# A one-core transformer step in fp32 on Trainium2: shorter routing, unread products, reordered waits, first weights in halves

## The chip, the cores and the metric

One core of a Trainium2 chip runs the whole program in one launch. The metric is device time in microseconds: the median of the runs, each from the first to the last instruction of the kernel.

## What is computed

The input is 256 tokens of width 1024 and a context of 256 tokens. The first block is an adaptively modulated layer with a gated delta net and a Fourier mixer, then a gated convolutional feed-forward. The second block has two layers: a short-convolution mixer or a linear recurrence, each followed by a mixture of 32 experts (two of one group of eight for each token) and a gate on an embedding. Cut to what matters for the change:

```python
mod_l = (silu_c @ w_ada[i] + b_ada[i])[:, None, :]
...
hl = modulate(rmsnorm(xl, g_pre_mix[i]), sh1l, sc1l)
hc = modulate(rmsnorm(xc, g_pre_mix[i]), sh1c, sc1c)
ul, zl, ql, kl, vl, bl, gl = mixer_inputs(hl, w_in[i], w_qkv_conv[i], a_log[i], dt_bias[i])
...
yl = mixer_out(ul, ol, zl, w_fourier[i], g_gdn[i], w_out[i])
xl = xl + gt1l * rmsnorm(yl, g_post_mix[i])
...
hl = modulate(rmsnorm(xl, g_pre_ffn[i]), sh2l, sc2l)
xl = xl + gt2l * rmsnorm(conv_ffn(hl, w_up[i], w_dwc[i], w_down[i], True), g_post_ffn[i])
...
pg = jax.nn.softmax((xf @ w_rg).astype(jnp.float32) + b_rg.astype(jnp.float32), axis=-1)
pg_top, g_top = lax.top_k(pg, 1)
le = ((xf @ w_re).astype(jnp.float32) + b_re.astype(jnp.float32)).reshape(n, N_GROUPS, EXPERTS_PER_GROUP)
le_sel = jnp.take_along_axis(le, g_top[:, :, None], axis=1)[:, 0]
...
hb = jax.nn.silu(xb @ w_gate[e]) * (xb @ w_up[e])
return hb @ w_down[e]
```

## The kernel before, in words

**Engines and semaphores.** Each engine has one hand-written instruction stream; semaphores join them. Activations lie transposed, as eight tiles (`k` = 0 to 7) of 128 channels by 256 tokens (512 with the context).

**Dense products.** A dense weight arrives by DMA in 2 MB chunks of 128x4096 (`w_in.0` is the first chunk of the mixer's input projection). ScalarE writes a rounded high part of each half chunk into ring slot 4 or 5 (L1403), and VectorE (L1980, `weights_low`) or GpSimd (L1865) then writes the remainder over the chunk; a table `by_dve` says which. The input is split in the same way: ScalarE writes the high part, VectorE the remainder (L1964, L1970, L2070). TensorE makes three products per `k` (`split_product`, L622): high by high, high by low, low by high. `projection` begins with `first_uses`, which takes `k` in the outer loop, so that each `k` needs only one new input tile; `together` says for how many of its two outputs both column tiles are made in that loop. The remaining outputs go through `dense_split`.

**The start.** TensorE computes the modulation (`ada_step`, L720 and L615), then the first uses of `w_in.0`, each `k` opened by three small rate products (L744, `ab_product`) for beta and decay. VectorE's order there is: scaled inputs of `k` 0 and 1 (L2075), the remainder of `w_in.0`'s first half, the low inputs of `k` 0 (L2070), and so on.

**The solve.** VectorE inverts a triangular matrix by a loop over columns and slips the modulation columns of later parts (`ada_columns`, L2201) in between; TensorE's `ada_step` products wait for these.

**Norms.** A residual is added tile by tile (L2005, L2008), ScalarE squares it (L1391), TensorE sums the squares over channels with a matrix of ones (L694), ScalarE makes the root (L1383, L1384), and VectorE and ScalarE make scaled, shifted, split inputs (L1993, L1426, L1412, L1964). The up-projection (`w_up`, 11 chunks) follows; its outputs go through a 3x3 convolution on VectorE. The down-projection has four pairs of output tiles, each tile of 22 steps of `k` (`n_k` = FT); `down_half` tells that the first tile's chunk is free.

**Experts.** In each of the two expert layers, 96 chunks of 2 MB (`q` = 0 to 95: per quad of four experts, four gates, four ups, four downs) run through ten places, in order, on one DMA queue issued by SyncE. `EXPERT_RINGS` says which place is which buffer; one place is made of two halves (`xnT` and `ple_w`), and its half in `ple_w` can be loaded only after the embedding products (`ple_mm`, L1054) have read it. Chunk `q` waits until chunk `q`-10 has been used (`consumed_by`). The first ten chunks are loaded while the mixer still runs. Routing lies between the mixer and the first gate product: logits (L1037), group and expert choice on VectorE (L2374 to L2412), ranks by products with a triangle of ones (L1083 to L1087), one-hot masks (L2429), and the gather of tokens by products (L1098). L1185 are the gate and up products, L1205 and L1262 products of the down-projections.

## Time and profile before

| | us |
|---|---|
| median of 3 runs (range) | 1683.92 (1681.86 to 1685.35) |
| the profiled execution | 1682.87 |
| its span in the trace | 1680.9 |
| TensorE busy | 1360.4 (81%) |
| VectorE busy | 593.0 (35%) |
| ScalarE busy | 433.9 (26%) |
| GpSimd busy | 219.8 (13%) |

The page says that the main DMA queue moved 525.22 MB and that the chain that ended last consists of TensorE for 53% and of DMA for 38%. Busy shares are means over stages with different limits. Idle time in brackets is time in which that engine had nothing to run, with what ended it.

### The profile page before, as it was taken

The numbers are of one execution on the slowest core, as the hardware profiler recorded it, in microseconds if no ns is written. First come the engines' busy times: TensorE is split into PE (matmuls) and PEld (weight loads), VectorE is DVE, ScalarE is ACT, GpSimd is POOL, SyncE is SP. The second block draws the span as 40 slices with busy tenths as digits, with TensorE's granted clock in tenths as the row PEclk, the third lists the DMA queues.
The fourth block names the chain that finished last, engine by engine and source line by source line (L and its number), as shares of the span: only waits on it lengthen the run. The fifth ranks groups of instructions, "written<-read, shape, count | busy, mean of one in ns | idle before, by whom it ended". The sixth has DMA issues, their size and how long they took to land.

```text
span 1680.9 us, 21875 instructions
## 1 busy us (share of the span) xinstructions
PE 1360.4 (81%) x9530; PEld 896.4 (53%) x9530; DVE 593.0 (35%) x1145; ACT 433.9 (26%) x655; POOL 219.8 (13%) x119
## 2 busy tenths in 40 slices
PE   5999998999999996776667567999966767666778
PEld 2797697999989961221222122998622212221226
DVE  2576723899437720110110011677201001101106
ACT  3445334544444320000000001665200000000005
POOL 0307322487430000000000000000000000000000
...
GB/s 402 127 59 164 202 113 201 115 187 154 157 216 151 373 316 428 427 428 426 427 428 425 429 425 412 232 163 362 273 427 427 427 426 428 426 427 427 427 410 99
DMA packets 51905, 528.40 MB, mean 314 GB/s; under 512 B 4704, under 2 KB 4832, under 8 KB 20064
## 3 DMA queue, kind: packets, MB, share of 16 engines
q1 hardware_dynamic: 51232, 525.22, 76.5%
...
HBM read 525.91 MB, written 1.05 MB: 313 GB/s over the span
## 4 chain that ended last, share of the span: by engine, by line
PE 53%; DMA 38%; DVE 4%; ACT 2%; SPq 2%; issue 1%; POOL 0%; DVEq 0%; ACTq 0%; POOLq 0%
PE bank L622 25%; DMA ring<-in_w_up 9%; PE bank L1185 9%; DMA ring<-in_w_gate 7%; DMA ring<-in_w_down 5%; DMA work<-in_w_down 5%; DMA work<-in_w_gate 5%; PE bank L1205 4%; DMA work<-in_w_up 4%; PE bank L1262 3%; PE bank L1330 2%; DMA ring<-in_dense 2%; PE bank L615 1%; PE bank L694 1%; SPq L524 1%; PE bank L1054 1%
## 5 line engine op out<-in xcount | busy, mean ns | idle before, releaser
L1185 PE MATMUL bank<-ring,work 128*32 128x512 f32 x1216 | 272.6, 737 | 142.3 <-DMA ring<-in_w_up 76.7
L622 PE MATMUL bank<-work_rounded,ring_rounded 128*128 128x256 f32 (+1 forms) x2032 | 317.8, 291 | 6.4 <-DVE xn_rounded L1970 3.5
L622 PEld LDWEIGHTS bank<-work_rounded,ring_rounded 128*128 128x128 f32 x2032 | 277.4, 189 | 15.9 <-issue 5.8
L622 PE MATMUL bank<-xn_rounded,ring_rounded 128*128 128x256 f32 (+1 forms) x1472 | 255.0, 291 | 3.4 <-DVE xn_rounded L1964 3.4
L1185 PEld LDWEIGHTS bank<-ring,work 128*32 128x32 f32 x1216 | 58.5, 131 | 322.2 <-issue 118.9
L622 PEld LDWEIGHTS bank<-xn_rounded,ring_rounded 128*128 128x128 f32 x1472 | 209.0, 194 | 7.7 <-issue 4.5
L2501 DVE TENSOR_TENSOR work<-work,bank 128x512 f32<-128x512 f32 x16 | 11.0, 689 | 569.8 <-PE bank L1185 569.8
L1865 POOL TENSOR_TENSOR ring_rounded<-ring,ring_rounded 128x2048 fp32r<-128x2048 f32 (+1 forms) x37 | 159.5, 4330 | 205.7 <-ACT ring_rounded L1403 205.7
L1185 PE MATMUL bank<-work 128*32 128x512 f32 x496 | 142.9, 688 | 32.7 <-DMA work<-in_w_gate 17.4
L1932 POOL TENSOR_TENSOR work<-work_rounded,work 128x128 f32<-128x128 f32 x32 | 12.1, 401 | 1071.5 <-PE bank L1237 738.6
L1403 ACT ACTIVATE ring_rounded<-ring 128x2048 fp32r<-128x2048 f32 (+1 forms) x78 | 136.5, 1796 | 51.5 <-PE bank L622 27.4
L1185 PE MATMUL bank<-spare,work 128*32 128x512 f32 x224 | 120.2, 738 | 22.3 <-DMA spare<-in_w_gate 14.6
L1205 PE MATMUL bank<-ring,work 128*32 128x512 f32 x576 | 100.6, 638 | 20.5 <-DMA ring<-in_w_down 20.5
L1980 DVE TENSOR_TENSOR ring_rounded<-ring,ring_rounded 128x2048 fp32r<-128x2048 f32 (+1 forms) x41 | 88.7, 2190 | 49.3 <-ACT ring_rounded L1403 49.1
L1185 PE MATMUL bank<-xn,work 128*32 128x512 f32 x112 | 73.4, 840 | 29.3 <-DMA work<-in_w_gate 20.0
L1725 ACT ACTIVATE work<-bank 128x512 f32<-128x512 f32 x16 | 9.6, 597 | 294.1 <-PE bank L1185 294.1
L1730 ACT ACTIVATE work<-bank 128x512 f32<-128x512 f32 x14 | 8.4, 600 | 293.5 <-PE bank L1098 293.5
L1205 PE MATMUL bank<-work 128*32 128x512 f32 x304 | 74.6, 649 | 11.5 <-DMA work<-in_w_down 11.5
L1185 PEld LDWEIGHTS bank<-work 128*32 128x32 f32 x496 | 32.5, 124 | 91.6 <-issue 44.0
L2511 DVE SCALAR_TENSOR_TENSOR xn_rounded<-bank,work,work_rounded 128x512 fp32r<-128x512 f32 x32 | 24.0, 751 | 160.0 <-ACT work_rounded L1738 160.0
L2293 DVE SCALAR_TENSOR_TENSOR work<-bank,params,work 128x189 f32<-128x189 f32 (+2 forms) x176 | 76.0, 432 | 6.2
L1098 PEld LDWEIGHTS bank<-work_rounded,work 128*128 128x128 f32 x512 | 58.5, 192 | 11.8 <-issue 11.7
...
## 6 DMA issues: line engine op xcount, KB each, us to landing
...
```

The costliest lines, as they stand in the source:

```text
L524: sp.dma_start(expert_columns(q, CHUNK // 4 * e, CHUNK // 4).rearrange("p (j n) -> p j n", j=2), columns[e])\
L622: last = mm(out, rv(high_store[r][:, at:at + P]), rv(x[part][k]), start=opens and k == 0 and j == 0, stop=closes and k == n_k - 1 and j == 2)
L1098: last = mm(out, xtok[:, u, k], rv(oneh[:, u].rearrange("p x s -> p (x s)")).bitcast(F32), start=u == 0, stop=u == NH - 1)
L1185: ins = mm(out[slots(y), :], xg[:, k, slots(y)], expert_columns(w, at, 512), start=k == 0, stop=k == KT - 1)
L1205: ins = mm(bank[6 + half][slots(y), :], hidT[:, j, slots(y)], expert_columns(w, at, 512), start=j == 0, stop=j == 3)
L1262: last = mm(bank[(use + b) % BANKS][:, SEQ * i:SEQ * i + SEQ], w[:, at:at + P], x[:, k], start=k == i == 0, stop=k == KT - 1 and i == 1)
L1330: last = mm(bank[(USE["out_b"] + b) % BANKS][:, SEQ * i:SEQ * i + SEQ], w[:, at:at + P], rr[0][:, k], start=k == i == 0, stop=k == KT - 1 ...
L1403: signal(act.activation(rv(high_store[HIGH_SLOT[n]][:, a:b]), w[:, a:b], ACT.Copy), "w_high")
L1865: pool.tensor_tensor(rv(w), w, rv(high_store[HIGH_SLOT[n]][:, a:b]), ALU.subtract).then_inc(S["w_low"], 1)
L1980: v.tensor_tensor(rv(w), w, rv(high_store[HIGH_SLOT[n]][:, a:b]), ALU.subtract).then_inc(S["w_low_dve"], 1)
L2293: ins = v.scalar_tensor_tensor(dst, x[:, r0 + dy:r1 + dy, c0 + dx:c1 + dx], par("w_dwc", 9 * f + 3 * (dy + 1) + dx + 1, 1), dst, ALU.mult, ...
L2511: ins = v.scalar_tensor_tensor(rv(y_low[half]), bank[6 + half][:].rearrange("p (k t) -> p k t", k=2), slot_w, rv(y_high[half]).rearrange(" ...
```

## The change

1. `w_in.0` is loaded as two DMAs of one half each (`half_full` tells the first); the remainder of its second half is made by GpSimd.
2. The rate weights' high and low parts lie side by side, so each `k` has two products of 32 rows; a product with a constant `fold` adds the two halves of the rows and transposes them.
3. `idle_products(n)`: TensorE makes n products of constants whose result nobody reads: 6 ahead of the first uses, 4 and 2 around the sums of squares ahead of the up-projection, 3 ahead of the short-convolution mixer (15 in all).
4. The mixer's output projection has `together=2`.
5. In the first pair of the down-projection, steps 0 to 19 of both tiles come before steps 20 and 21 of both.
6. In the norm ahead of the up-projection, ScalarE writes only the high part (with the shift in its bias), and VectorE makes the low part in one instruction.
7. Modulation columns move to earlier places around the solve.
8. Routing: the tokens are the stationary operand, so the logits come out with tokens in rows; the copy, the transposes and several VectorE steps go. The rank products are signalled after three of five, the weights come after the first one-hot masks, and only two of the eight column tiles of the embedding products stay ahead of the first gate; the other six follow the first quad's ups.
9. Place 5 is now ring 5 and place 9 the two halves; the second half of `q` = 9 waits for the embedding products in the loop, ahead of `q` = 14. A few small waits and signals follow from this.

```diff
-EXPERT_RINGS = (0, 1, None, None, None, None, 2, 4, 3, 5)
+EXPERT_RINGS = (0, 1, None, None, None, 5, 2, 4, 3, None)
...
-    halved = tuple(first[f"ple{layer}"] for layer in range(2))
-    whole = (*halved, first["w_in_b"])
+    halved = (first["w_in"], *(first[f"ple{layer}"] for layer in range(2)))
+    whole = (*halved[1:], first["w_in_b"])
...
-        ("w_in", (0, 3, 4)), ("w_out", (1,)), ("w_up", (1,)), ("w_in_a", range(1, 6)), ("w_out_a", range(2)), ("ple0", (1,)),
+        ("w_in", (3, 4)), ("w_out", (1,)), ("w_up", (1,)), ("w_in_a", range(1, 6)), ("w_out_a", range(2)), ("ple0", (1,)),
...
-    by_dve += [(first["w_down"] + c, 0) for c in range(2, 8)] + [(first["w_in_a"], 0)]
+    by_dve += [(first["w_in"], 0)] + [(first["w_down"] + c, 0) for c in range(2, 8)] + [(first["w_in_a"], 0)]
...
             sp.wait_ge(S["tok_mm"], 4 * (layer + 1))
-            expert(5, 0)
-            sp.wait_ge(S["ple_mm"], 4 * (layer + 1))
-            expert(5, 1)
+            expert(9, 0)
...
+                if q == EXPERT_SLOTS + TOGETHER:
+                    sp.wait_ge(S["ple_mm"], EMBEDS * (layer + 1))
+                    expert(9, 1)
...
+            both = ready is not None and n_k == FT
+            parts = (range(n_k - 2), range(n_k - 2, n_k)) if both else (range(n_k),)
+            for part in parts:
+                for i, (chunk, tile) in enumerate(tiles):
+                    for k in part:
...
+        def idle_products(count):
+
+            for _ in range(count):
+                mm(bank[6][:], ones, consts[:, 0:4 * P], start=True, stop=True)
+
...
+        idle_products(6)
...
-            for j, (w, x) in enumerate(((0, 0), (0, 1), (1, 0))):
-                last = mm(bank[7][0:16, :], rv(w_ab[w][:, k]), rv(both[x][k]), start=k == 0 and j == 0,
-                          stop=k == KT - 1 and j == 2)
+            for x in range(2):
+                last = mm(bank[7][0:32, :], rv(w_abs[:, k].rearrange("p s c -> p (s c)")), rv(both[x][k]), start=k == 0 and x == 0,
+                          stop=k == KT - 1 and x == 1)
...
         sum_squares(late)
+        idle_products(4)
         ready = norm_input()
+        idle_products(2)
         projection("up", "w_up", FT, xparts, ready, together=1)
...
-                last = mm(bank[7][0:36, 0:SEQ], w_r[:, layer, k], xs[k], start=k == 0, stop=k == KT - 1)
+                for u in range(NH):
+                    last = mm(bank[6][:, LOGITS * u:LOGITS * u + LOGITS], xs[k][:, P * u:P * u + P], w_r[:, layer, k],
+                              start=k == u == 0, stop=k == KT - 1 and u == 1)
...
+                    signal(v.scalar_tensor_tensor(rv(xnT[:, k - 2]), xnT[:, k - 2], mod[:, 24 + k - 2, 0:1], rv(rounded[:, k - 2]),
+                                                  ALU.add, ALU.subtract), "xn_ready")
...
-            if k == 4:
-                weights_low(FIRST["w_in"], (1,))
...
-        for m in range(1, 5):
-            ada_columns(2, m)
+        for m in range(2, 5):
+            columns_added(2, m)
```

**What moves on VectorE and GpSimd at the start.** The names: `ring0` is `w_in.0`, whose high parts lie in `ring4`; `xn` and `hT` with `gains` are the scaled inputs, `xn_rounded<-xn,mod,work_rounded` the low inputs of a `k` (two instructions for each `k`). VectorE before:

```order
L1980 TENSOR_TENSOR ring0_rounded_49<-ring0,ring4_rounded_53 128x2048 [waits w_high]
L2070 SCALAR_TENSOR_TENSOR xn_rounded_55<-xn,mod,work_rounded_57 128x256 [waits x_high]
L2070 SCALAR_TENSOR_TENSOR xn_rounded_55<-xn,mod,work_rounded_57 128x256
L2075 SCALAR_TENSOR_TENSOR xn<-work,gains,bank5 128x256
L2075 SCALAR_TENSOR_TENSOR xn<-hT,gains,bank5 128x256
L2070 SCALAR_TENSOR_TENSOR xn_rounded_55<-xn,mod,work_rounded_57 128x256 [waits x_high]
L2070 SCALAR_TENSOR_TENSOR xn_rounded_55<-xn,mod,work_rounded_57 128x256
L2075 SCALAR_TENSOR_TENSOR xn<-work,gains,bank5 128x256
L2075 SCALAR_TENSOR_TENSOR xn<-hT,gains,bank5 128x256
L1980 TENSOR_TENSOR ring0_rounded_49<-ring0,ring4_rounded_53 128x2048 [waits w_high]
L2070 SCALAR_TENSOR_TENSOR xn_rounded_55<-xn,mod,work_rounded_57 128x256 [waits x_high]
```

VectorE now:

```order
L1995 TENSOR_TENSOR ring0_rounded_49<-ring0,ring4_rounded_53 128x2048 [waits w_high]
L2088 SCALAR_TENSOR_TENSOR xn_rounded_55<-xn,mod,work_rounded_57 128x256 [waits x_high]
L2088 SCALAR_TENSOR_TENSOR xn_rounded_55<-xn,mod,work_rounded_57 128x256
L2093 SCALAR_TENSOR_TENSOR xn<-work,gains,bank5 128x256
L2093 SCALAR_TENSOR_TENSOR xn<-hT,gains,bank5 128x256
L2088 SCALAR_TENSOR_TENSOR xn_rounded_55<-xn,mod,work_rounded_57 128x256 [waits x_high]
L2088 SCALAR_TENSOR_TENSOR xn_rounded_55<-xn,mod,work_rounded_57 128x256
L2093 SCALAR_TENSOR_TENSOR xn<-work,gains,bank5 128x256
L2093 SCALAR_TENSOR_TENSOR xn<-hT,gains,bank5 128x256
L2088 SCALAR_TENSOR_TENSOR xn_rounded_55<-xn,mod,work_rounded_57 128x256 [waits x_high]
```

The second remainder has left VectorE's queue, where it stood behind the low inputs of `k` 1 and 2. GpSimd's queue at its start, now:

```order
L1867 MEMSET work 128x256
L1879 ISA
L1879 TENSOR_TENSOR ring0_rounded_49<-ring0,ring4_rounded_53 128x2048 [waits w_high]
L1879 TENSOR_TENSOR ring1_rounded_50<-ring1,ring5_rounded_54 128x2048 [waits w_high] x2
L1879 TENSOR_TENSOR ring2_rounded_51<-ring2,ring4_rounded_53 128x2048 [waits w_high] x2
```

It stands there first, ahead of the four remainders of the next two chunks, which were first before.

**What moves on TensorE around the norm ahead of the up-projection.** `bank4<-xn,consts` are the sums of squares, `xn_rounded_55,ring5_rounded_54` the first products of the up-projection. Before:

```order
L694 MATMUL bank4<-xn,consts 128x256
L694 MATMUL bank4<-xn,consts 128x256 [waits sq_ready]
L694 MATMUL bank4<-xn,consts 128x256
L694 MATMUL bank4<-xn,consts 128x256 [waits sq_ready]
L694 MATMUL bank4<-xn,consts 128x256
L694 MATMUL bank4<-xn,consts 128x256 [waits sq_ready]
L694 MATMUL bank4<-xn,consts 128x256
L694 MATMUL bank4<-xn,consts 128x256 [waits sq_ready]
L694 MATMUL bank4<-xn,consts 128x256
L622 MATMUL bank2<-xn_rounded_55,ring5_rounded_54 128x256 [waits xn_ready,w_low,dense_free3,dense_free2]
```

Now:

```order
L718 MATMUL bank6<-consts 128x512 x4
L708 MATMUL bank4<-xn,consts 128x256 [waits sq_ready]
L708 MATMUL bank4<-xn,consts 128x256
L708 MATMUL bank4<-xn,consts 128x256 [waits sq_ready]
L708 MATMUL bank4<-xn,consts 128x256
L708 MATMUL bank4<-xn,consts 128x256 [waits sq_ready]
L708 MATMUL bank4<-xn,consts 128x256
L708 MATMUL bank4<-xn,consts 128x256 [waits sq_ready]
L708 MATMUL bank4<-xn,consts 128x256
L718 MATMUL bank6<-consts 128x512 x2
L632 MATMUL bank2<-xn_rounded_55,ring5_rounded_54 128x256 [waits xn_ready,w_low,dense_free3,dense_free2]
L632 MATMUL bank2<-xn_rounded_55,ring5_rounded_54 128x256
```

The two rows `bank6<-consts`, of four and of two products, are new; the others keep their order.

**What moves on TensorE in the routing of the first expert layer.** `bank5<-work,consts 128x32` are ranks, `work_rounded_57,work 128x128` the gather, `work 128x256` the embedding products, `ring0,work` the first gate. Before:

```order
L1054 MATMUL bank7<-work 128x256 x4
L1083 MATMUL bank5<-work,consts 128x32 [waits mask_ready]
L1084 MATMUL bank5<-work,consts 128x32
L1085 MATMUL bank5<-work,consts 128x32
L1086 MATMUL bank5<-work,consts 128x32
L1087 MATMUL bank5<-work,consts 128x32
L1054 MATMUL bank0<-work 128x256 [waits tok_sb]
L1054 MATMUL bank0<-work 128x256 x3
L1098 MATMUL bank2<-work_rounded_57,work 128x128 [waits onehot,tok_sb]
L1098 MATMUL bank2<-work_rounded_57,work 128x128 x7
L1098 MATMUL bank3<-work_rounded_57,work 128x128 x8
L1054 MATMUL bank6<-work 128x256 x4
```

Now:

```order
L1078 MATMUL bank4<-work 128x256 [waits ple_w_load,mask_load]
L1078 MATMUL bank4<-work 128x256
L1100 MATMUL bank5<-work,consts 128x32 [waits mask_ready]
L1101 MATMUL bank5<-work,consts 128x32
L1102 MATMUL bank5<-work,consts 128x32
L1103 MATMUL bank7<-work,consts 128x32
L1104 MATMUL bank7<-work,consts 128x32
L1113 MATMUL bank2<-work_rounded_57,work 128x128 [waits onehot,tok_sb]
L1113 MATMUL bank2<-work_rounded_57,work 128x128 x7
L1113 MATMUL bank3<-work_rounded_57,work 128x128 x8
L1078 MATMUL bank6<-work 128x256 x2
```

Ahead of the first of these rows before stands another pair of embedding tiles (`bank4`, four instructions). Of the four pairs that stood ahead of the first gate, two single tiles are left there (two instructions each); the other six follow the first quad's ups.

## Rows read from the trace of the kernel before

**Rows 1.** The page: gigabytes per second in 40 slices of the span.

```profile
GB/s 402 127 59 164 202 113 201 115 187 154 157 216 151 373 316 428 427 428 426 427 428 425 429 425 412 232 163 362 273 427 427 427 426 428 426 427 427 427 410 99
```

**Rows 2.** The chain that ended last, the first products: start, length, work.

```profile
24.40 12.37 DMA ring<-in_dense
...
45.89 0.69 PE bank L744 x3
46.58 1.39 PE bank L622 x6
```

**Rows 3.** Timeline of the start: start, length, engine, line, tiles, [idle before <- releaser].

```profile
36.80 1.91 ACT L1403 ACTIVATE ring_rounded<-ring 128x2048 fp32r<-128x2048 f32 x1 [12.99 <-DMA ring<-in_dense]
...
38.74 2.29 DVE L1980 TENSOR_TENSOR ring_rounded<-ring,ring_rounded 128x2048 fp32r<-128x2048 f32 x1 [2.02 <-ACT ring_rounded L1403]
40.21 1.90 ACT L1403 ACTIVATE ring_rounded<-ring 128x2048 fp32r<-128x2048 f32 x1
40.95 0.88 DVE L2070 SCALAR_TENSOR_TENSOR xn_rounded<-xn,mod,work_rounded 128x256 fp32r<-128x256 f32 x2
...
41.97 0.58 PE L744 MATMUL bank<-work_rounded 128*16 128x512 f32 x1 [7.52 <-DVE xn_rounded L2070]
```

**Rows 4.** Windows: busy (x instructions) by engine, granted clock, DMA share, GB/s.

```profile
18.00:21.00 3.00, 3.00 (x7) 1.18 (x7) 0.00 (x0) 0.00 (x0) 0.00 (x0) 1.00 1.01 431
297.00:300.00 3.00, 3.00 (x16) 3.00 (x15) 2.33 (x7) 2.69 (x9) 0.00 (x0) 0.50 0.00 0
```

**Rows 5.** Timeline behind the triangular solve, TensorE.

```profile
194.82 2.02 PE L615 MATMUL bank<-consts,work 128*128 128x128 f32 x16 [1.79 <-DVE mod L2201]
```

**Rows 6.** Timeline ahead of the second half of the mixer's output projection.

```profile
246.30 4.54 POOL L1865 TENSOR_TENSOR ring_rounded<-ring,ring_rounded 128x2048 fp32r<-128x2048 f32 x1
...
249.06 3.06 DVE L1964 TENSOR_TENSOR work_rounded<-work,work_rounded 128x256 fp32r<-128x256 f32 x4 [4.28 <-ACT work_rounded L1412]
...
258.64 3.55 PE L622 MATMUL bank<-work_rounded,ring_rounded 128*128 128x256 f32 x28 [1.45 <-DVE work_rounded L1964]
```

**Rows 7.** Timeline around the norm ahead of the up-projection.

```profile
285.74 6.51 PE L694 MATMUL bank<-xn,consts 128*128 128x256 f32 x16 [3.57 <-ACT xn L1391]
...
289.03 0.63 ACT L1391 ACTIVATE xn<-hT 128x512 f32<-128x512 f32 x1 [0.43 <-DVE hT L2008]
...
295.61 9.61 PE L622 MATMUL bank<-xn_rounded,ring_rounded 128*128 128x256 f32 x56 [3.36 <-DVE xn_rounded L1964]
```

**Rows 8.** The chain through the up-projection.

```profile
295.61 129.91 PE bank L622 x1056
```

**Rows 9.** Timeline at the start of the down-projection.

```profile
434.01 11.19 PE L622 MATMUL bank<-work_rounded,ring_rounded 128*128 128x256 f32 x92 [1.47 <-DVE work_rounded L1964]
...
435.10 2.66 ACT L1403 ACTIVATE ring_rounded<-ring 128x1408 fp32r<-128x1408 f32 x2 [2.40 <-PE bank L622]
```

**Rows 10.** Windows at the short-convolution mixer's first projection, columns as in rows 4.

```profile
493.00:496.00 3.00, 0.19 (x1) 0.00 (x0) 1.89 (x6) 1.32 (x3) 0.00 (x0) 1.00 0.72 306
496.00:499.00 3.00, 2.30 (x11) 2.33 (x12) 3.00 (x10) 2.22 (x5) 0.00 (x0) 0.54 0.74 311
```

**Rows 11.** Timeline of the first expert layer's routing and first experts.

```profile
602.49 3.62 PE L1054 MATMUL bank<-work 128*128 128x256 f32 x16
...
605.38 0.23 DVE L2412 TENSOR_TENSOR work<-work 128x64 f32<-128x64 f32 x1
...
608.78 3.73 PE L1098 MATMUL bank<-work_rounded,work 128*128 128x128 f32 x32
...
614.18 3.64 PE L1185 MATMUL bank<-ring,work 128*32 128x512 f32 x32
614.28 0.38 SPq L533 DMA_DIRECT2D work<-in_w_up  x1
...
616.16 2.06 SPq L536 DMA_DIRECT2D ring<-in_w_down  x2
```

**Rows 12.** The same place in the second expert layer.

```profile
1206.44 3.64 PE L1185 MATMUL bank<-ring,work 128*32 128x512 f32 x32
```

240 lines of the change are left out of this document (116 added, 124 removed).

## Prediction

> **What bounds the kernel now.** I read first how many bytes move when [rows 1]. In slices 16 to 24 and 30 to 38 the DMA queue moves 427 GB/s: these are the two expert layers, and there the kernel ends as early as its stream of 2 MB chunks does, 4.92 us for each. Elsewhere the chain that ended last is TensorE's work with a few waits in it. So two kinds of edit can gain: one that shortens a wait of TensorE outside the expert layers, and one that makes the expert stream start earlier. A us saved in TensorE's work inside the stream is worth nothing. Then I read the chain and the timeline at each place that the change touches: at the start, the wait for `w_in.0` [rows 2, 3]; behind the solve [rows 5]; in the output projection [rows 6]; around the norm and the up-projection [rows 7, 8]; at the down-projection [rows 9]; at the next mixer [rows 10]; and in the routing [rows 11, 12]. A saving ahead of an expert layer passes through it whole, since the stream goes on when places come free.
>
> **The start.** Before, `w_in.0` lands at 36.77 [rows 2]; ScalarE's high part starts at 36.80, VectorE's remainder at 38.74, the low inputs at 40.95, TensorE at 41.97 after 7.52 us idle [rows 3]. The DMA engines are full there (431 GB/s [rows 4]), so a half of 1 MB takes 2.43 us and the first half lands at 34.35. ScalarE: 1.91 to 36.25. VectorE's scaled inputs are done by then (its order starts the remainder behind four of them), remainder 36.75 to 39.05, low inputs 0.88 to 39.95: TensorE starts at 40.0, 2.0 earlier. The six unread products fill 34.45 to 39.6: seven records of such a product fit in 3.00 us [rows 4], two records each, so 0.86 each, 5.2 in all. They cost nothing as long as the input is not earlier than 39.6.
>
> Now the second half. ScalarE starts its high part 3.41 after the first (36.80 to 40.21 [rows 3]), so at 37.8, to 39.7. GpSimd then makes its remainder, 4.54 us by [rows 6], from 39.9 to about 44.4. What is beside it: VectorE's low inputs of `k` = 1, due at 40.7, which read two operands from SBUF. In [rows 6] four such instructions begin at 249.06 and take 3.06 us, and GpSimd's remainder ends at 250.84: 1.78 us of them are the wait for GpSimd, the four themselves 1.28, 0.32 each. So I let the low inputs of `k` = 1 wait until 44.4 and end at 45.25, and TensorE starts `k` = 1 at 45.3, after 3.4 us idle. The other steps: a `k` takes 2.08 now, 0.69 for three rate products and 1.39 for six others [rows 2]; with two rate products 1.85. End of the first uses: 45.3 + 7 x 1.85 = 58.25, against 41.97 + 3.92 + 7 x 2.08 = 60.45 (the first `k` takes 3.92 at the low clock, 41.97 to 45.89). Gain 2.2; if the idle time brings the clock down again, one `k` costs 1.84 more and 0.36 is left. Idle stretches of about that length do bring it down elsewhere: the 3.36 us ahead of 295.61 are followed by a granted clock of 0.50 (1.2 GHz) [rows 4, 7]. I take **0.4**, near that end. Without the wait for GpSimd TensorE never stops: 40.0 + 8 x 1.85 = 54.8, gain 5.65. Bounds 0 and 5.65.
>
> The Trainium skill has a rule that speaks against this edit ("SBUF — State Buffer", section "Who interferes with whom"): a VectorE instruction with two SBUF inputs and a GpSimd instruction that reads SBUF exclude each other, and the later one is blocked for the whole of the earlier one. The trace agrees [rows 6]. By that rule the start gains 0.4 to 2.2; with two engines that don't disturb each other it would be 5.65, and the whole sum 18.8.
>
> **Behind the solve.** TensorE's 1.79 us ahead of 194.82 are a wait for the modulation columns L2201, which stand on VectorE behind the two large transposes [rows 5]. Now they are made inside the column loop, before them; the loop gets one in and gives one up. TensorE goes straight on: **1.8**. If the solve's own results are late next, less; bounds 1.2 and 1.8.
>
> **Output projection.** The 1.45 us ahead of 258.64 wait for the fifth `cat` tile [rows 6]. `together=2` puts 24 products more ahead of that wait, at 129.91 / 1056 = 0.123 us each [rows 8] 2.9 us of work that was to do anyway: **1.45**. Bounds 1.0 and 1.45.
>
> **Norm and up-projection.** Three terms. (a) The sums of squares take 6.51 us for eight products (16 records) behind 3.57 us idle, at the low clock [rows 7]. With four unread products (3.4 us) inside those 3.57 the clock stays high; then the end is set by the last squares, 289.03 + 0.63 = 289.66, plus the last four records, 0.24 each: 290.6 instead of 285.74 + 6.51 = 292.25. Gain 1.65. (b) The chain from the root to the first low input loses one ScalarE pass and a handover. A pass over 512 columns takes 0.63 [rows 7]; for 256 and the handover together I estimate 0.65. (c) 56 products take 9.61 us from 295.61; at 0.12 each (129.91 less these 2.9 us, over 1056) it would be 6.75. VectorE's low inputs come every 0.9 us at most (two instructions a `k`, 0.44 each by the pair of 0.88 in [rows 3]) against 1.08 us of TensorE's nine products per `k`, so TensorE keeps its pace. Gain 2.8 if two unread products (1.7 of the 2.7 us gap that is left) keep the clock up. Together **5.1**; bounds 2.3 (a and b alone, or c alone) and 5.3.
>
> **Down-projection.** The 1.47 us ahead of 434.01 [rows 9] are now filled by the second tile's steps, but the first tile ends later: before at 434.01 + 6 x 0.12 = 434.7; now at 432.54 + 60 x 0.12 + 0.7 = 440.45. Behind it waits ScalarE's high part of the third chunk (435.10, waiting for TensorE; 1.33 each), then VectorE's remainder of 1408 columns (2.29 x 1408 / 2048 = 1.6 by [rows 3]), then the second pair. 440.8 + 1.33 + 1.6 = 443.8. Before, the second pair starts at 434.01 + 72 x 0.12 = 442.6. So the wait comes back larger: **-1.2**. Bounds -3 (the clock drops in the 2.6 us gap) and +1.4.
>
> **Next mixer.** From 496.7, 11 products take 2.30 us at a mean clock of 0.54 [rows 10], and the idle time before is over 3 us; at 0.12 they take 1.3, and some more follow at the low clock: **1.3** if the three unread products (2.6 us) hold it. Bounds 0 and 1.5.
>
> **Routing, twice.** The first gate product starts at 614.18 [rows 11]. Ahead of the mask (605.38) go the logits' copy, two transposes and some seven VectorE instructions of its size (0.23): seven of 0.2 and some 0.7 for copy, transposes and handovers put the mask at about 603.4. Three rank products, ranks and one-hot masks take 1.9 (608.78 less 605.6, less the 1.3 for which the gather stood behind embedding products): gather from 605.3, 3.73 long, then one tile of embedding products (3.62 for four tiles, 0.9): gates at 610.0, 4.2 earlier. But what counts is the stream. Before, SyncE issues the second half of its split chunk at 614.28 and `q` = 10 at 616.16, behind it; 614.31 + 2.46 = 616.77 is when the stream proper can start. Now `q` = 10 goes 1.98 us behind the first gate, at 612.0, with nothing ahead; the half chunk comes later, inside the stream: 612.0 + 2.46 = 614.4. Gain 2.35, not 4.2. The second layer has the same pattern, gates at 1206.44 [rows 12]: **4.7** together. Its condition: all chunks from 14 on queue behind SyncE's wait for the embedding products. These end at 610.0 + 13.8 (four times 3.45 [rows 11]) + 5.3 = 629.1; chunks 10 to 13 keep the queue busy until 612.0 + 4 x 4.92 = 631.7. 2.6 us to spare. Bounds per layer 0 and 4.2.
>
> **Nothing for the rest.** The wider parameters (some 45 KB) are 0.1 us; the transposes by `fold` replace four others; the moved split in the up stage has TensorE-bound work over it.
>
> **Sum.** 0.4 + 1.8 + 1.45 + 5.1 - 1.2 + 1.3 + 4.7 = 13.55 us. The terms are from an execution of 1682.87 us (span 1680.9), which is 1.05 below the median of the runs, 1683.92. In that frame: 1670.4.
>
> **Rivals.** A: the low inputs don't wait for GpSimd at the start. For it: later low inputs in the trace are often made without harm, and the wait needs the overlap at just this place. Against: [rows 6]. 5.25 more (5.65 for 0.4): **1665.1**, chance 0.15. B: the unread products don't hold the clock (too few for the gaps that are left). Then (c) 2.8 and the next mixer's 1.3 are lost and the down-projection's gap costs 1 more: 8.45 gained, **1675.5**, chance 0.2. For it: the clock is still 0.5 from 297 to 300, well after TensorE has resumed. The Trainium skill ("TensorE: Matmul & The Clock Gate", Part 1, "What's actually happening") says that the lower clock is the default and that activity of the array releases it; unread products should then do as well as others, which no row here shows. C: the mask is earlier by less, or the embeddings end some 2 us late, and the stream starts as before: 4.7 lost, **1675.1**, chance 0.06. D, the slower side: SyncE's wait ahead of `q` = 14. If ScalarE frees the banks of the six late tiles only behind the first quad's hidden products, the queue runs dry in both layers. Each us beyond the 2.6 to spare costs one per layer; the change is slower by over 0.2% (3.4 us, about what a measurement of this kernel can tell from none) from 11 us late on. At 12 us late: 13.55 - 2 x 9.4 = 5.3 slower, **1689.2**, chance 0.03. For it only that the wait is new; against, that ScalarE has 0.60 us copies there and little else. E: the terms eat each other up and less than 3.4 us is left: 0.03. The forecast keeps 0.53.
>
> **Range.** The forecast's own is 1667 to 1674. With A and B in it: 1662.5 to 1677.5 holds some 8 in 10. Faster 0.93, within 0.2% 0.04, slower 0.03.
>
> **What would show it.** At the start: GpSimd's remainder beside low inputs that take some 4 us, TensorE idle over 3 us behind the first `k`, first uses ending at 58 to 60. L2201's wait and the 1.45 us gone. The granted clock near 1 from 290 to 300 in the norm. A wait of some 2.6 us ahead of the second pair of the down-projection. First gate some 4 us nearer to the last logits, `q` = 10 right behind, no gap in the queue at `q` = 14. I am wrong most likely at the start (A), at the clock, or where a wait that I took for hidden comes out.

## The result and the profile after

| | before | after |
|---|---|---|
| median (range), us | 1683.92 (1681.86 to 1685.35) | 1674.47 (1673.04 to 1677.23) |
| the profiled execution, us | 1682.87 | 1675.44 |
| its span, us | 1680.9 | 1673.3 |

The ratio of the medians is 0.9947, with a 95% interval of 0.9933 to 0.996: 9.45 us faster, where 13.55 was forecast. The profiled execution of before was 1.05 below its median, that of after is 0.97 above, so the two traces show only 7.6 us. Page of after (busy time of the engines, granted clock in tenths, GB/s in 40 slices):

```profile
PE 1377.9 (82%) x9584; PEld 914.9 (55%) x9584; DVE 592.4 (35%) x1130; ACT 432.0 (26%) x647; POOL 225.4 (13%) x120
...
PEclk9999889999999997887887788999988878878889
...
GB/s 402 131 55 161 211 106 210 151 166 140 166 209 152 376 327 427 426 429 428 428 427 429 427 426 413 237 160 361 284 428 428 428 428 427 428 427 426 428 412 109
```

The expert stream is as full as in [rows 1]; it begins earlier. I laid the starts of the same TensorE instruction in the two traces beside each other; "lead" is how much earlier it starts now, "own part" how much of that arose since the row above.

| place (time in after) | lead, us | its own part | forecast |
|---|---|---|---|
| end of the first uses (59.65) | 0.85 | 0.85 | 0.4 |
| modulation products behind the large transposes (191.94) | 2.88 | +2.0 | +1.8 |
| output projection (252.3) | 0.03 | -2.85 | 0 |
| sums of squares end (280.87) | 1.31 | +1.3 | +1.45 |
| up-projection, two `k` on (295.4) | 5.5 | +4.2 | +5.1 |
| down-projection, third pair (458) | 2.8 | -2.7 | -1.2 |
| next mixer, first products (494.40, then 496) | 2.3, then 3.3 | -0.5, +1.0 | 0, +1.3 |
| first routing, gather (604.64) | 4.1 | +1.36, and -0.5 ahead of it | +2.35 |
| second routing, gather (1194.84) | 6.2 | +1.30, and +0.8 ahead of it | +2.35 |
| end (1673.3) | 7.6 | +1.4 | 0 |

The own part of a routing is what the stretch from the first one-column sum to the first gather product got shorter: 21.73 to 20.37 us, and 17.84 to 16.54.

Two rows need care. The 0.85 us of the start don't last: at 159.8 both traces stand level (159.79 before, 159.81 now). The 2.88 at 191.94 come from behind that place: a wait of 1.65 us for modulation columns at 168.39 is gone (lead 1.9), a wait for a DMA of 0.81 at 175.24 is new (lead 1.0), and the 1.79 of [rows 5] are gone. And a lead is the difference of two single executions, which differ by themselves. Seven traces of this study, that of after among them, share every instruction of the changed start: their eighth `k` (`k` = 7) begins anywhere from 56.00 to 59.03. The product in the row of 252.3 begins at 251.1 to 255.1 in the six of them that share the solve too, and at 251.1 to 253.1 in the four traces with the old start and solve. So ahead of that row the change gains nothing that these traces show.

**The start.** Timeline of after, columns as in [rows 3]:

```profile
34.46 5.32 PE L718 MATMUL bank<-consts 128*128 128x512 f32 x12
...
36.81 2.28 DVE L1995 TENSOR_TENSOR ring_rounded<-ring,ring_rounded 128x2048 fp32r<-128x2048 f32 x1
...
39.73 4.55 POOL L1879 TENSOR_TENSOR ring_rounded<-ring,ring_rounded 128x2048 fp32r<-128x2048 f32 x1 [38.68 <-ACT ring_rounded L1422]
...
40.03 0.39 PE L763 MATMUL bank<-work_rounded 128*32 128x512 f32 x1 [0.26 <-DVE xn_rounded L2088]
...
40.59 4.38 DVE L2088 SCALAR_TENSOR_TENSOR xn_rounded<-xn,mod,work_rounded 128x256 fp32r<-128x256 f32 x2
...
45.02 0.42 PE L763 MATMUL bank<-work_rounded 128*32 128x512 f32 x1 [3.00 <-DVE xn_rounded L2088]
```

The two low inputs of `k` = 1 take 4.38 us instead of 0.88 [rows 3]: they end 0.7 behind GpSimd's remainder. TensorE stands still for 3.00 us.

**The granted clock.** Windows of after, columns as in [rows 4]:

```profile
42.00:45.00 3.00, 0.03 (x1) 0.00 (x0) 3.00 (x3) 0.00 (x0) 2.29 (x1) 1.00 1.00 426
45.00:48.00 3.00, 2.98 (x8) 2.10 (x9) 3.00 (x8) 1.55 (x4) 0.00 (x0) 0.59 1.01 431
...
199.00:202.00 3.00, 2.57 (x73) 2.60 (x75) 0.54 (x1) 1.38 (x4) 2.88 (x5) 0.53 0.03 5
...
283.00:286.00 3.00, 2.54 (x9) 1.02 (x8) 3.00 (x9) 1.26 (x2) 0.00 (x0) 1.00 0.92 393
...
289.00:292.00 3.00, 2.25 (x7) 0.89 (x5) 1.55 (x4) 1.85 (x5) 0.00 (x0) 1.00 0.00 0
...
298.00:301.00 3.00, 3.00 (x28) 3.00 (x27) 2.96 (x2) 2.98 (x3) 0.00 (x0) 1.00 0.00 0
435.00:438.00 3.00, 0.55 (x5) 0.35 (x3) 1.63 (x1) 3.00 (x4) 0.34 (x1) 1.00 0.66 188
438.00:441.00 3.00, 2.88 (x13) 2.92 (x14) 1.15 (x1) 3.00 (x4) 3.00 (x1) 0.52 1.00 371
493.00:496.00 3.00, 2.06 (x15) 1.63 (x14) 3.00 (x10) 2.06 (x4) 0.00 (x0) 1.00 0.92 393
496.00:499.00 3.00, 3.00 (x27) 2.97 (x26) 3.00 (x9) 2.27 (x5) 0.00 (x0) 1.00 0.01 5
...
586.00:589.00 3.00, 3.00 (x26) 3.00 (x26) 0.00 (x0) 0.00 (x0) 0.00 (x0) 0.88 1.01 416
589.00:592.00 3.00, 3.00 (x17) 3.00 (x17) 0.00 (x0) 0.00 (x0) 0.00 (x0) 0.55 0.64 258
...
446.00:458.00 12.00, 12.00 (x102) 12.00 (x101) 1.62 (x1) 4.94 (x6) 3.40 (x1) 1.00 0.47 143
```

Three readings. Around the norm and in the next mixer the clock is now 1.00, where it was 0.50 and 0.54 [rows 4, 10]. Behind the two idle gaps (42 to 45, 435 to 438) it falls to 0.59 and 0.52, that is to 1.2 GHz for most of the window. The second fall is in all eight traces with that gap; the first is not in each: in experiments 4 and 9 the same idle time of 2.99 us stands at the same place, and the clock stays at 1.00, as the first line of the window rows of experiment 4 shows. And it falls in the routing (589 to 592) although TensorE is busy all the time. Before, the same window reads

```profile
589.00:592.00 3.00, 3.00 (x19) 2.01 (x18) 0.00 (x0) 0.00 (x0) 0.00 (x0) 1.00 1.03 423
```

**Norm and down-projection.** The chain of after that ended last:

```profile
292.40 127.68 PE bank L632 x1059
...
434.93 1.39 ACT ring_rounded L1422
...
436.34 1.64 DVE ring_rounded L1995
...
438.12 33.40 PE bank L632 x264
...
473.24 15.83 PE bank L632 x132
```

The up-projection starts 3.2 earlier (1.3 of that from the output projection) and takes 2.2 less than in [rows 8] (127.68 for three records more). Ahead of 438.12 stands the new wait of 2.57 us, exactly the two passes of which the prediction spoke.

**Solve and routing.** Timeline of after:

```profile
191.94 2.05 PE L625 MATMUL bank<-consts,work 128*128 128x128 f32 x16
...
192.69 1.28 ACT L1456 ACT_TABLE_LOAD   x1
...
194.88 3.93 PE L910 MATMUL bank<-ring,xn 32*32 32x32 f32 x128 [0.89 <-DVE ring L2236]
...
195.06 1.28 ACT L1456 ACT_TABLE_LOAD   x1
...
198.69 1.07 ACT L1586 ACTIVATE ring<-bank 32x512 f32<-32x512 f32 x2
...
199.43 0.23 PE L922 MATMUL bank<-ring 32*32 32x32 f32 x1 [0.62 <-ACT ring L1586]
...
585.98 1.96 PE L1060 MATMUL bank<-params,xn 128*128 128x40 f32 x16
...
604.64 3.81 PE L1113 MATMUL bank<-work_rounded,work 128*128 128x128 f32 x32 [0.57 <-DVE work_rounded L2428]
...
609.28 3.64 PE L1199 MATMUL bank<-ring,work 128*32 128x512 f32 x32
...
611.26 2.04 SPq L545 DMA_DIRECT2D ring<-in_w_down  x2
```

At 191.94 the wait of [rows 5] is gone. But the solve's own results are next: VectorE's second transpose (0.89 us), then ScalarE with two table loads of 1.28 us (0.62 us). The first gate is 4.90 earlier than in [rows 11], `q` = 10 too, 1.98 behind it as before.

### The profile page after: what moved, and what is told of

Its sections match the earlier page's. It is cut to its first block, busy times and chain, and to the rows that moved or that the text cites. A ratio compares the mean times of both kernels' runs of the same rounds, so it can differ in the third digit from the quotient of the medians.

```text
span 1673.3 us, 21964 instructions
## 1 busy us (share of the span) xinstructions
PE 1377.9 (82%) x9584; PEld 914.9 (55%) x9584; DVE 592.4 (35%) x1130; ACT 432.0 (26%) x647; POOL 225.4 (13%) x120
## 3 DMA queue, kind: packets, MB, share of 16 engines
q8 instruction: 78, 1.28, 0.3%
HBM read 525.95 MB, written 1.05 MB: 315 GB/s over the span
## 4 chain that ended last, share of the span: by engine, by line
PE 54%; DMA 38%; SPq 3%; ACT 2%; DVE 2%; issue 1%; POOL 0%; DVEq 0%; ACTq 0%; POOLq 0%
PE bank L632 26%; PE bank L1199 9%; DMA ring<-in_w_up 7%; DMA work<-in_w_gate 7%; DMA ring<-in_w_down 7%; DMA ring<-in_w_gate 5%; DMA work<-in_w_down 4%; DMA ring<-in_dense 4%; PE bank L1219 4%; DMA work<-in_w_up 4%; SPq L533 3%; PE bank L1281 3%; PE bank L625 2%; PE bank L1349 2%; PE bank L819 1%; PE bank L708 1%
## 5 line engine op out<-in xcount | busy, mean ns | idle before, releaser
L1199 PE MATMUL bank<-ring,work 128*32 128x512 f32 x1248 | 319.8, 727 | 134.0 <-DMA ring<-in_w_up 71.9
L632 PE MATMUL bank<-work_rounded,ring_rounded 128*128 128x256 f32 (+1 forms) x2032 | 322.1, 294 | 3.5 <-DVE ring_rounded L1995 2.6
L632 PEld LDWEIGHTS bank<-work_rounded,ring_rounded 128*128 128x128 f32 x2032 | 282.0, 193 | 12.4 <-issue 5.9
L1199 PEld LDWEIGHTS bank<-ring,work 128*32 128x32 f32 x1248 | 70.2, 130 | 306.0 <-issue 109.4
L1879 POOL TENSOR_TENSOR ring_rounded<-ring,ring_rounded 128x2048 fp32r<-128x2048 f32 (+1 forms) x38 | 165.2, 4364 | 196.5 <-ACT ring_rounded L1422 196.3
L1199 PE MATMUL bank<-work 128*32 128x512 f32 x480 | 153.9, 687 | 31.3 <-DMA work<-in_w_gate 15.7
L1219 PE MATMUL bank<-ring,work 128*32 128x512 f32 x576 | 127.8, 677 | 18.4 <-DMA ring<-in_w_down 18.4
L1199 PE MATMUL bank<-spare,work 128*32 128x512 f32 x224 | 115.5, 716 | 17.8 <-DMA spare<-in_w_gate 7.7
L1219 PE MATMUL bank<-work 128*32 128x512 f32 x304 | 88.8, 662 | 12.1 <-DMA work<-in_w_down 12.1
L1199 PE MATMUL bank<-xn,work 128*32 128x512 f32 x96 | 69.7, 884 | 25.7 <-DMA work<-in_w_up 14.2
L1199 PEld LDWEIGHTS bank<-work 128*32 128x32 f32 x480 | 37.3, 124 | 92.5 <-issue 46.2
L1752 ACT ACTIVATE work_rounded<-bank,work 128x512 fp32r<-128x512 f32 x32 | 22.0, 688 | 166.3 <-PE bank L1219 166.3
```

What stands on the lines that cost most here:

```text
L632: last = mm(out, rv(high_store[r][:, at:at + P]), rv(x[part][k]), start=opens and k == 0 and j == 0, stop=closes and k == n_k - 1 and j == 2)
L1199: ins = mm(out[slots(y), :], xg[:, k, slots(y)], expert_columns(w, at, 512), start=k == 0, stop=k == KT - 1)
L1219: ins = mm(bank[6 + half][slots(y), :], hidT[:, j, slots(y)], expert_columns(w, at, 512), start=j == 0, stop=j == 3)
L1879: pool.tensor_tensor(rv(w), w, rv(high_store[HIGH_SLOT[n]][:, a:b]), ALU.subtract).then_inc(S["w_low"], 1)
```

## The experiments

Each kernel was run beside the kernel before (whose median was 1682.9 to 1683.5), 4 to 12 executions each. The interval of a ratio is about 2 us to either side, and medians of two kernels within some 2 us aren't told apart, so for small edits I read the trace at the place too; a trace shows one execution.

**1. The two-tile order in the down-projection undone.**

```diff
-            both = ready is not None and n_k == FT
+            both = False
```

> Only the order of the first down-projection pair goes back to that of before. Theory 1 (the edit costs, since the first tile's chunk comes free later and the wait comes back as a larger one with a clock drop behind it): the 2.2 us or so of idle time ahead of the second pair go, 1.5 us come back ahead of steps 20 and 21, TensorE is 2 to 3 us earlier in the next mixer, and the whole is 2 to 3 us faster than the changed kernel, near 1672. Theory 2 (the loss there belongs to the earlier arrival of TensorE at that place, whatever the order): no difference beyond 1 us.

Measured: 1672.43, ratio 0.9941 (0.9928 to 0.9953): 2.0 below the changed kernel. Timeline, TensorE:

```profile
430.15 16.10 PE L632 MATMUL bank<-work_rounded,ring_rounded 128*128 128x256 f32 x132 [1.31 <-DVE work_rounded L1979]
```

The 1.31 us ahead of the last steps are back, no wait follows, and the clock doesn't fall. Counted from the first product of the up-projection, the next mixer starts 199.3 us on, against 202.0 in the changed kernel: this part of the change loses 2.7 us, where the forecast said 1.2. The median agrees (2.0), though by itself it wouldn't be clear of the noise.

**2. The second remainder of `w_in.0` back on VectorE.**

```diff
-        ("w_in", (3, 4)), ...
+        ("w_in", (0, 3, 4)), ...
+            if k == 4:
+                weights_low(FIRST["w_in"], (1,))
```

> w_in.0 is still loaded in halves, but the remainder of the second half is made by VectorE, at the place in its order where it stood before. Theory 1 (GpSimd's remainder blocks VectorE's low inputs for 4 us and brings TensorE's clock down): the low inputs of k = 1 take 0.9 us and not 4.4, TensorE goes on after its first k, and the first uses end at about 55.5, against 59.7 in the changed kernel. Theory 2 for what it is worth in the end: the 4 us pass through, near 1670.5; its rival: other waits ahead of the delta net take it up, as they took up 0.9 us in the changed kernel, and the whole is within 1.5 us of the changed kernel.

Measured: 1672.69, ratio 0.9945 (0.9932 to 0.9958), span 1670.8. Timeline:

```profile
40.90 0.87 DVE L2090 SCALAR_TENSOR_TENSOR xn_rounded<-xn,mod,work_rounded 128x256 fp32r<-128x256 f32 x2
...
42.19 0.39 PE L763 MATMUL bank<-work_rounded 128*32 128x512 f32 x1
```

The low inputs of `k` = 1 take 0.87 us again, TensorE doesn't wait (42.19 instead of 45.02), `k` = 7 starts 2.84 earlier, and in this trace 2.5 us of it reach the end. The 4.38 us are GpSimd's doing. What they cost in the end is less sure: `k` = 7 starts 1.2 to 4.2 earlier than in the seven traces named above, the row of 252.3 (249.99 here) 1.1 to 5.1 earlier than in the six, and the medians differ by 1.8.

**3. The fifteen unread products left out** (nobody reads them, so the output is the same).

```diff
-            for _ in range(count):
+            for _ in range(0):
```

> All 15 unread products are left out. Theory 1 (they hold the clock around the norm and ahead of the next mixer, and cost nothing): granted clock 0.5 again from some 3 us after the start of the gap ahead of the sums of squares, the up-projection's first 56 products 9.6 us again, 4 to 5.5 us slower than the changed kernel, near 1679.5. Theory 2 (the clock comes back by itself or they hide nothing): within 1 us of the changed kernel.

Measured: 1676.05, ratio 0.9963 (0.9951 to 0.9975): 1.6 above the changed kernel, far less than the 1679.5 of my theory. Windows:

```profile
45.00:48.00 3.00, 2.90 (x13) 2.16 (x14) 3.00 (x9) 1.47 (x4) 0.00 (x0) 1.00 1.02 437
...
283.00:286.00 3.00, 3.00 (x11) 2.44 (x10) 2.27 (x7) 1.67 (x3) 0.00 (x0) 0.65 0.14 60
...
292.00:295.00 3.00, 3.00 (x27) 3.00 (x27) 2.55 (x7) 2.44 (x4) 0.00 (x0) 1.00 0.00 0
493.00:496.00 3.00, 3.00 (x17) 3.00 (x16) 3.00 (x9) 1.78 (x4) 0.00 (x0) 0.55 0.12 44
```

Without them the clock is 0.65 under the sums of squares and 0.55 in the next mixer. The mixer pays for it: 91.4 us from its first product to the first one-column sum, against 89.9. The norm doesn't: from the row of 252.3 to the first product of the up-projection it is 40.18 us, against 40.08, since the last squares set the end of the sums. And the up-projection starts at full clock all the same. So in this trace the 2.8 us that the prediction gave to the clock in the up-projection need no unread product. With them the clock is 1.00 there in ten traces of ten; without them it is low in the three with the old norm (before, experiment 5 and `a2_before_fill`) and not here, so a single trace carries this reading. The start says nothing on them: `k` = 7 begins at 56.13 here, and at 56.00 in experiments 4 and 9, which have the unread products.

**4. One unread product of 512 columns between the sums and the router's products.**

```diff
+            idle_products(1, 7)
```

> One unread product of 512 columns stands between the one-column token sums and the router's 40-column products, at both places of both layers (four in all, 3.4 us of TensorE). Theory 1 (the stretches of one-column and 40-column products alone let the clock fall, which costs about 1.5 and 0.9 us in each layer): with them the granted clock stays near 1 from the first router products to the gather, and the time is 0 to 2 us better than the changed kernel in spite of the added work. Theory 2 (the clock falls for another reason): the clock falls as before and it is 2 to 3.4 us slower.

Measured: 1680.43, ratio 0.9987 (0.9975 to 0.9998), 6 us above the changed kernel. Windows:

```profile
45.00:48.00 3.00, 3.00 (x14) 2.22 (x15) 3.00 (x8) 1.59 (x4) 0.00 (x0) 1.00 1.02 437
...
589.00:592.00 3.00, 3.00 (x16) 3.00 (x16) 0.00 (x0) 0.00 (x0) 0.00 (x0) 0.50 0.19 78
```

The clock fell all the same and for longer (0.59, 0.50, 0.77 in the three windows from 586, 0.88, 0.55, 1.00 without). This remedy is refuted. It adds 3.4 us of TensorE work by its own count. The rest is the lower clock: in the second layer it stays at 0.50 from 1185 to 1200, and sums to gather take 23.18 us instead of 16.54. (The traced execution is 3.4 us above the median of its kernel.)

**5 to 7. Parts alone: only the routing on the kernel before; everything but the routing; only the norm's edits (unread products 4 and 2, high part only on ScalarE) on the kernel before.** The first takes over

```diff
-EXPERT_RINGS = (0, 1, None, None, None, None, 2, 4, 3, 5)
+EXPERT_RINGS = (0, 1, None, None, None, 5, 2, 4, 3, None)
...
+                for u in range(NH):
+                    last = mm(bank[6][:, LOGITS * u:LOGITS * u + LOGITS], xs[k][:, P * u:P * u + P], w_r[:, layer, k],
...
+                if q == EXPERT_SLOTS + TOGETHER:
+                    sp.wait_ge(S["ple_mm"], EMBEDS * (layer + 1))
```

> The kernel before with the routing part alone (items 8 and 9: logits, routing steps, embeddings, the swapped places). Theory 1 (each layer's stream starts 2.4 us earlier by the prediction's account, and some 3.2 by the changed kernel's trace, although the router's narrow products let the clock fall): 5 to 7 us faster than before. Theory 2 (the clock loss eats the routing gain and the time comes from elsewhere): within 2.5 us of before.

> The changed kernel without the routing part (all that stands ahead of the first expert layer's routing). Theory 1 (the parts add up; ahead of routing only some 3 us are left of the 8.85 forecast): 2 to 4 us faster than before. Theory 2 (the forecast's 8.85 us ahead of routing are there and the routing part is what falls short): 7 to 9 us faster than before.

> The kernel before with the edits around the norm ahead of the up-projection alone (four and two unread products, one ScalarE pass less). Theory 1 (the prediction's: sums 1.65, chain 0.65, clock 2.8): 4.5 to 5 us faster than before, granted clock near 1 from 285 to 303. Theory 2 (the clock there depends on where its falls and rises lie, and comes back without help in some executions, as it did in the kernel without unread products): 2 to 3 us faster.

Measured: only the routing 1676.80 (ratio 0.9961, 0.9948 to 0.9975); without the routing 1673.88 (0.9944, 0.993 to 0.9957); only the norm 1679.97 (0.9982, 0.9973 to 0.9991). The gains, about 6.5 and 9.5, add up to 16 where the whole has 9. In the trace the routing alone is worth 2.9 us (sums to gather 20.18 and 16.52 us against 21.73 and 17.84). The norm's edits bring the up-projection 3.24 us forward, then 5.46 behind its first products; 1.29 of both were there at the row of 252.3 already, so their own worth is 1.95, then 4.2, as in the whole. So the local terms do add up; something else sets the medians, and it is not in the list of the change.

**8. Where the `work` area lies.** The moving operands of the output and down-projections lie in one SBUF area, `work`, allocated behind the parameters. Wider parameters push it back, by 4 bytes a column: in the changed kernel by 88 columns. The distances between the starts of such products, at a granted clock of 1.00, go with the place, but not with it alone. The last column is the fourth pair of output tiles, which reads the same operand behind some products for the sums of squares:

| kernel | `work` further on than before, bytes | mean distance at 450 to 465, ns | products in 446 to 458 | mean distance in the fourth pair, ns |
|---|---|---|---|---|
| before | 0 | 118.7 | 104 | 117.3 |
| only the norm | 0 | 117.3 | 104 | 117.3 |
| `a2_before_fill` | 32 | 113.3 | 108 | 117.8 |
| without routing | 64 | 118.3 | 104 | 118.3 |
| only routing | 288 | 113.3 | 108 | 113.3 |
| changed kernel | 352 | 120.0 | 102 | 120.0 |
| `a1_shift192` | 544 | 113.3 | 109 | 113.3 |
| all remedies (experiment 11) | 544 | 113.3 | 109 | 113.3 |

In the experiments on the changed kernel that leave the place alone it is 120.0 again, in both columns. The up-projection reads `xn`, which is allocated ahead of the parameters, and has a median of 120.0 in every kernel. Two of the kernels in the table were made for this question; they change the place of `work` and of what is allocated behind it, and nothing that is computed: `a1_shift192` is the changed kernel with `gains` allocated ahead of `work` and eight unread constant columns (192 bytes), `a2_before_fill` the kernel before with the eight columns (32 bytes).

```diff
-    ("iota1", SLOTS), ("eps", 1),
+    ("iota1", SLOTS), ("eps", 1), ("fill", 8),
```

> The changed kernel with the large work area moved up by 192 bytes in SBUF (a small tile allocated ahead of it, and 8 unread columns of constants); not one instruction more or less. In the traces so far the dense products of 256 columns that read that area follow each other every 118.7 ns in the kernel before, every 120.0 in the changed kernel and its variants, and every 113.3 in the one with routing alone, where that area stands 288 bytes from its place before; here it stands at the same place modulo 256. Theory 1 (the place of the moving operand sets the pitch): 113.3 ns in the down-projection's steady part, 2 to 4 us faster than the changed kernel. Theory 2 (the instruction stream or the execution sets it): 120.0 ns, no difference beyond 1 us.

> The kernel before with 8 unread columns of constants more, which moves the work area by 32 bytes, to the same place modulo 256 as in the kernel with routing alone. Theory 1 (place sets the pitch): 113.3 ns in the down-projection, 2 to 4 us faster than before. Theory 2: 118.7 ns as before, no difference beyond 1 us.

Measured: a1 1672.15, ratio 0.9933 (0.992 to 0.9947), 2.3 below the changed kernel; a2 1680.94, ratio 0.9989 (0.998 to 0.9998), some 2 us below the kernel before. Both have a distance of 113.3 ns from 450 to 465. Window and chain of a2, then chain of a1:

```profile
446.00:458.00 12.00, 12.00 (x108) 12.00 (x108) 1.63 (x1) 5.01 (x6) 5.19 (x2) 1.00 0.49 151
...
472.30 15.55 PE bank L622 x132
```

```profile
438.91 31.49 PE bank L632 x264
...
472.13 14.98 PE bank L632 x132
```

The same 396 records take 46.47 us here and 49.23 in the changed kernel (33.40 and 15.83 above): 2.76 us with nothing changed but where buffers lie. a2 against the kernel before, which compute the same, shows it too in the first three pairs (108 products against 104; 38.37 us for 336 records against 40.14), but not in the fourth: 15.55 us for 132 records against 15.49, where `a1_shift192` and the routing alone take 14.98. And the kernel before has two distances, 118.7 and 117.3, with the operand at one place. So a move of the buffers changes the distance by up to 6.7 ns, and all seven traces at 352 bytes have 120.0 throughout; but within one execution a stretch can take another value than the one ahead of it, and what picks it isn't known.

**9. Router products between dense ones.**

```diff
-                dense_split(*tiles(b), x)
+                jobs = ahead() if ahead and b == uses - 1 else []
+                dense_split(*tiles(b), x, jobs=jobs)
...
+                        if jobs and k % 2 == 1 and not (i and k == n_k - 1):
+                            jobs.pop(0)()
```

> The changed kernel with its first layer's early token sums and router products put one by one between the dense products of the last output tile, and one group of token transposes between the late router products and the late token sums in both layers. No work is added. Theory 1 (rows of narrow products one after another let the clock fall): in the first layer the granted clock stays near 1 from 583 to 600 and TensorE is 1.5 to 2.5 us earlier at the first gate; 1.5 to 2.5 us faster than the changed kernel. Theory 2 (the narrow products lower the clock even when they are mixed with wide ones, or something else does): no gain, or less than 0.5 us.

Measured: 1675.09 (1673.35 to 1678.84), ratio 0.9959 (0.9946 to 0.9973). Windows:

```profile
589.00:592.00 3.00, 3.00 (x27) 3.00 (x27) 0.00 (x0) 0.00 (x0) 0.00 (x0) 1.00 0.67 272
```

The clock stays at 1.00 from 583 to 601, and sums to gather take 17.64 and 14.82 us, 2.7 and 1.7 less than in the changed kernel (in the second layer only the token products stand between the router's). That looks like theory 1, but it isn't shown. The clock falls later instead, to 0.58 from 604 to 607, in the gather itself:

```profile
602.92 5.44 PE L1118 MATMUL bank<-work_rounded,work 128*128 128x128 f32 x32 [0.57 <-DVE work_rounded L2433]
```

The gather takes 5.44 us instead of 3.81, and the first gate starts at 609.18, against 609.28 in the changed kernel. And the kernel of experiment 10, whose routing is that of the changed kernel, with 16 one-column and 16 40-column products in a row from 587.09 to 590.6, has the same shape without any product moved:

```profile
589.00:592.00 3.00, 3.00 (x28) 3.00 (x28) 0.00 (x0) 0.00 (x0) 0.00 (x0) 1.00 1.01 416
```

There sums to gather take 18.00 and 14.86 us, and its gather too takes 5.44. From the first sum to the first gate it is 23.90 and 19.46 us in experiment 9, 24.27 and 19.50 in experiment 10, 25.01 and 21.18 in the changed kernel. So how often the clock falls in a layer's routing, and where, differs between executions of the same instructions, and the mixed order isn't shown to be worth anything. The profiled span is 2.1 us shorter than that of the changed kernel, the median no shorter.

**10. The modulation columns back in their old places.**

```diff
-        columns_added(1, 1)
...
-            if j in (9, 14, 18):
-                columns_added(1, (9, 14, 18).index(j) + 2)
-            if j == 28:
-                columns_added(2, 1)
+            if j in (1, 9, 14, 18):
+                ada_columns(1, (1, 9, 14, 18).index(j) + 1)
```

> The changed kernel with the modulation columns at their old places around the solve (item 7 undone). Theory 1 (ScalarE's two table loads and its copies behind the modulation products set the end of the solve, so moving VectorE's columns gains nothing but an earlier fall of the clock in the 32x32 products): TensorE waits 1.8 us for the columns again, the first products that read the solved halves start within 0.3 us of where they do in the changed kernel, and the time is within 1 us of it. Theory 2 (the prediction's: the wait was worth 1.8 us): 1.5 to 2 us slower, near 1676.

Measured: 1675.45, ratio 0.9962 (0.9948 to 0.9975), 1.0 above the changed kernel, which the runs can't tell from it. Timeline, TensorE:

```profile
168.52 2.08 PE L625 MATMUL bank<-work 128*128 128x128 f32 x8 [2.54 <-DVE mod L2219]
...
202.05 0.18 PE L922 MATMUL bank<-ring 32*32 32x32 f32 x1 [1.06 <-ACT ring L1586]
```

I expected less than 0.3 us at the place and was wrong: the columns at their old places make TensorE wait at 168.52, and the products behind the solve start 2.62 later than at 199.43 (in the other kernels with the changed start and the moved columns they start at 198.7 to 201.4, so some of the 2.62 is the spread). The other wait for columns, 1.79 us in [rows 5], is 0.46 here, at 195.10, where I had expected 1.8. The moved columns have a price: in the nine traces that have them the clock falls between 193.2 and 199.2, in the five with the old places between 199.4 and 202.7.

**11. All remedies in one**: experiments 1, 2, 9 and `a1` together.

> The changed kernel with the down-projection's old order, the second remainder of w_in.0 on VectorE, narrow router products put between others, and the work area moved as in a1. If the parts add up (2.0 and 1.8 by the medians so far, 3 us for the routing by the traces, 2 to 4 for the place if theory 1 holds): 1665 to 1668; without an effect of the place 1668 to 1671.

Measured: **1664.97** (1664.63 to 1666.98), ratio 0.9894 (0.9878 to 0.9909), span 1662.9: some 18 us faster than before by the ratio, 9.5 faster than the changed kernel, and the fastest kernel of this study. Windows:

```profile
446.00:458.00 12.00, 12.00 (x109) 12.00 (x108) 1.63 (x1) 4.73 (x5) 5.46 (x2) 1.00 0.50 170
...
589.00:592.00 3.00, 3.00 (x16) 2.78 (x16) 2.69 (x20) 2.06 (x4) 0.00 (x0) 0.66 0.92 385
```

The span is 7.9 us shorter than that of `a1_shift192`, which lacks the three other remedies; 6.0 of it are there at the next mixer (486.40 against 492.44), from the start and the down-projection. The mixed order of the router products doesn't hold the clock here (0.66 in the second window; the routing lies earlier in this kernel). Sums to gather take 18.06 and 16.50 us, against 20.44 and 16.52 in `a1_shift192`, and experiment 10 has 18.00 without the mixed order. So the sum came out at the edge of the forecast, but the 3 us that I had put down to the router products aren't shown to be theirs.

## Why the prediction came out as it did

The time fell into the range and the direction was right. Of the waits most went as told; four terms had the wrong size, one effect of up to 2 to 3 us was not in the prediction at all, and that the time fell into the range is in part luck, since the spread of single executions at one place is as large as most terms.

- **Start: right in the wait for GpSimd, by luck in the 40.0.** Forecast were a wait of GpSimd's length, 3.4 us idle, the low clock behind it, first uses ending at 58 to 60; measured 4.38, 3.00, 0.59, 59.65. The rule of the Trainium skill ("SBUF — State Buffer", "Who interferes with whom") holds here by the 4.38 us. Rival A is refuted; experiment 2 puts its worth at 2.8 us at the place and 2.5 at the end of its trace, with the spread told there. TensorE's first product came at 40.03 as forecast, but not by the way forecast: the first half landed by 33.18, over 1 us earlier, and VectorE's remainder (36.81, forecast 36.75) waited for its four scaled inputs, which need the modulation that TensorE ends at 34.6. By this trace a smaller first piece would have gained nothing more. And the 0.85 us gained are gone at 159.8.
- **Solve, 1.8: the wait went, its gain did not stay.** The step "TensorE goes straight on" failed. Next come the solve's results (0.89 and 0.62 us), and the clock falls earlier in the 32x32 products (0.53 from 199 to 202, where it was 1.00 before), which takes the lead of 1.01 at 199.43 to about nothing (0.03 at 252.3). What the moved columns are good for is an earlier wait, at 168, which I had overlooked (1.65 us in the trace of before, 2.54 in experiment 10).
- **Output projection, 1.45: right** (1.3).
- **Norm and up-projection, 5.1: 4.2.** (a) and (b) gave 1.9 (forecast 2.3), (c) 2.3 (forecast 2.8). The reason for (a) and (c) isn't borne out: experiment 3 has the norm as short and the full clock in the up-projection without any unread product. Rival B, that they don't hold the clock, is out (1.00 from 283 to 301, in all ten traces with them); but all fifteen are worth 1.6 us by the medians, which is within the noise, and 1.5 by the trace, all of it in the next mixer.
- **Down-projection, -1.2: -2.7.** The wait was foreseen (2.6, measured 2.57), and the fall of the clock stood in the bound (-3), not in the value. I had seen an idle gap bring the clock down in my own rows (3.36 us in [rows 7], over 3 us ahead of [rows 10]) and didn't apply it.
- **Next mixer, 1.3: right** (1.0; experiment 3 loses 1.5 there).
- **Routing, 4.7: 2.7.** Two steps failed. The first gate was to come 4.2 us earlier by its own means; it came 4.9 earlier, but 2.8 of that lead was there at the first sum. And the clock falls in the new routing (1.00 before, 0.88 and 0.55 now, with TensorE busy for 3.00 of 3.00 us), which makes the first layer's stretch up to the gather 2.4 us longer than in experiment 10's trace, where the same instructions keep the clock up to there. All ten traces with the router's new 40-column products have one fall or more in each layer's routing, the four with the old 256-column ones none; the one-column sums are in both, so they alone don't do it. No experiment takes the fall away. The reckoning by SyncE's half chunk doesn't hold either: with a gate 2.1 us earlier by its own means it would leave 0.3 of the 2.35, and the stream gained 1.3. From the start of the gather to the 170th megabyte of DMA twelve of the fourteen traces take 130.7 to 131.3 us (experiments 9 and 10, with the low clock in the gather, 132.6 and 132.7), so the stream gains what the gather gains. Rival D didn't occur: the DMA engines have no gap at `q` = 14. That leaves C half true: the gather, and the stream with it, is earlier by less.
- **Not in the sum: the place of `work`.** I costed the wider parameters at 0.1 us. They cost 1.3 ns for each product that reads `work`, against the first three pairs of before, and hide 6.7 ns that another place gives (experiment 8). Together with the spread between executions this can explain why the two halves of the change don't add up. How much of 16 - 9 is place and how much is spread stays open.

The own parts in the table come to 5.4 us up to the second gather; 2.2 us more of lead (0.8 ahead of the second routing, 1.4 behind it) arise inside stretches where the same work is done, and 2 us are the place of each profiled execution within its own runs. That part isn't settled.
